# An unread fp32 product and four unread transposes at three places of a TensorE-bound kernel

## The chip, the cores and the metric

The kernel runs on one core of one Trainium2 chip. The metric is the device time of one execution in microseconds. A core has TensorE (PE, matrix products, with its weight loads listed apart as PEld), VectorE (DVE), ScalarE (ACT), GpSimd (POOL) and SyncE (SP), which here issues the DMAs.

## The reference

Two blocks on 256 tokens of width 1024, all fp32. The first has modulated feed-forward layers around a mixer that joins a short convolution and grouped-query attention; the second has an even layer (mLSTM heads and stick-breaking heads) and an odd layer (pooling windows, a mixing product, a gated projection):

```python
def reference(...):
    x = first_block(x, c, ctx, c_ctx, ...)      # 256 latent and 256 context tokens
    return second_block(x, ...)

def first_block(...):
    x = x + 0.5 * ml[2] * swiglu(modulate(rms_norm(x, norm1_g), ml[0], ml[1]), ffn1_w_in, ffn1_w_out)
    ...
    o_l = latent_attention(q_l, k_all, v_all)
    x = x + ml[5] * merge_branches(y_conv_l, o_l, gt_l, w_branch_conv, w_branch_attn, w_out)
    x = x + 0.5 * ml[8] * swiglu(modulate(rms_norm(x, norm3_g), ml[6], ml[7]), ffn2_w_in, ffn2_w_out)
    return rms_norm(x, final_g)

def odd_layer(...):
    ...
    y = (mixed * silu(z)) @ w_out
    return x + rmsnorm(y, post_g)
```

## The kernel before

Activations are kept transposed: features on the 128 partitions, tokens in the columns. Every large product is a `gemm`: two output tiles of 128 features from a strip of 256 weight columns, over `nk` slices of 128 features. The weights come in chunks of up to four slices (512 KB) through a ring `W` of eight buffers by SyncE. Each chunk is split into a high and a low part: ScalarE writes the high part `WH` (L1458), VectorE the rest `WL` (L1863). The activations are split in the same way (`XHB` and `XLB`, `GH` and `GL`, `OH` and `OL`, `YH` and `YL`, `RH` and `RL`). A slice is then three matmuls of 128x128 weights with 256 moving columns: high by high (L1038), high weights by low activations (L1039), low weights by high activations (L1040), 48 for a gemm with `nk` = 8 and 96 for one with `nk` = 16. They go to four PSUM banks in turn (0 to 3).

A planner (`Plan`) writes one list of steps, and each engine's program walks through it and does its share of each step. `prog` is a list of calls that make these steps; `gemm` and `call` append to it. Small work (attention, heads) is written as generators in `self.back`, which `tick` takes turns with, twice for each chunk. It uses the PSUM banks 4 to 6 in rotation: `bank` hands out the next one with the semaphore value at which the last user freed it, and TensorE waits on that value before the step.

TensorE works in the order of the list. Around the three places that order is: the attention is drained (`drain`), then the four gemms `ma` (attention branch, from 642.5 us), the four gemms `res` (w_out, to 688 us), a norm with some unread products of constants that bridge it (`warm`, L1057), then the second feed-forward block (`ffn(2, ...)`, from 694 us to 886 us: pairs of gemms `fa2` and `fb2`, and `fx2`); much later, from 1299.5 us, the four gemms `p1` (output projection of the odd layer, `nk` = 16), and the final norm.

Two steps of the attention have the shapes of the added ones: `score` (L1142), one fp32 product with 512 moving columns, and `turn` (L1147), four fp32 transposes of 128x128 into one bank. `gather` (L1154) is four fp32 products with 256 columns. An fp32 product appears in the trace as two records, a transpose as one.

```python
                elif s.kind == "turn":
                    pe.wait_ge(S["ap"], s.a + 1)
                    for c in range(4):
                        mm = pe.transpose(ps[:, c * 128:c * 128 + 128], TS[:, s.a % 3, c * 128:c * 128 + 128], con("id"))
                    mm.then_inc(S["atp"], 1)
```

Of the kernel before, what the change touches and what calls it, by code (L numbers as in the profile page):

```python
# [122 lines left out]
class Plan:  # L123
# [30 lines left out]
    def bank(self, freed):  # L154
        b = 4 + self.uses % 3
        self.uses += 1
        before = self.bank_free.get(b)
        self.bank_free[b] = freed
        return b, before

    def load(self, src, nk, freed):
        self.loads.append((src, nk, freed))
        return len(self.loads) - 1
# [364 lines left out]
    def build(self):  # L528
# [56 lines left out]
        self.call(self.drain)  # L585
        for i in range(4):
            self.gemm("ma", i, w["w_branch_attn"], 0, 8, 256 * i, (0, T), first=i == 0)
        self.call(self.stats, "s3")
        for i in range(4):
            self.gemm("res", i, w["w_out"], 0, 8, 256 * i, (0, T), first=i == 0, norm=i == 3)  # L590
# [37 lines left out]
        for g in range(4, 8):  # L628
            c = 5128 + 256 * (g - 4)
# [39 lines left out]
        self.call(self.stats, "s7")  # L669
        for i in range(4):  # L670
            self.gemm("p1", i, w["w_out_c_2"], 0, 16, 256 * i, (0, T), first=i == 0, norm=i == 3)
        self.call(self.post, 1)

    def ended(self, *name):
# [14 lines left out]
    def ffn(self, n, win, wout, cols):  # L689
        a, b = cols  # L690
        for f0, f1 in ((0, 12), (12, 22)):
            for f in range(2 if n == 1 and f0 == 0 else f0, f1, 2):
                self.gemm(f"fa{n}", f, win, 0, 8, f * 128, cols, first=f == 0)
                self.gemm(f"fb{n}", f, win, 0, 8, DFF + f * 128, cols)
            if f0 == 0:
                self.call(lambda: self.step("gates", a=n))
            else:
                self.call(self.ended, "hx", n)
                self.call(self.stats, "s2" if n == 1 else "s4")
            for m in range(0, 8, 2):  # L700
                if n == 1 and f0 == 12 and m == 6:
                    self.halves(wout, f0 * 128, f1 - f0, m * 128)
                    continue
                self.gemm(f"fx{n}", m, wout, f0 * 128, f1 - f0, m * 128, (0, b - a), g=f0, first=m == 0)
            self.call(self.ended, "fx", n, f0)
# [79 lines left out]
    def gates(self, bank):  # L785
        self.step("g0", bank=bank)
        for _ in range(5):
            yield
        self.step("g1", bank=bank)
        for _ in range(3):  # L790
            yield
        self.step("g2")
        for _ in range(8):
            yield
        b, f = self.bank(("att", 1))
        self.step("g4", bank=b, free=f)
        self.ready.add("att")
# [45 lines left out]
def build_program(nc, w, out):  # L843
    with ExitStack() as ctx:
# [12 lines left out]
        def sbuf(st, name, shape, dt=F32):  # L857
            return st.enter_context(nc.sbuf_tensor(name, shape, dt))

        V = sbuf(ctx, "V", [128, NVEC])  # L860
        C = sbuf(ctx, "C", [128, NCON])
# [62 lines left out]
        def con(name, a=0, b=None, rows=128):  # L924
            s, e = CON[name]
            return C[0:rows, s + a:(e if b is None else s + b)]
# [36 lines left out]
        @block.sync  # L963
        def _(sp):
            sp.dma_start(X[:, :, 256:512], w["xt"].rearrange("(k p) t -> p k t", p=128)).then_inc(SI[2], 16)
            sp.dma_start(X[:, :, 0:256], w["ctxt"].rearrange("(k p) t -> p k t", p=128)).then_inc(SI[3], 16)
            for i, (src, m, _) in enumerate(plan.loads):
                if i >= WR:
                    for name, v in plan.loads[i - WR][2]:
                        sp.wait_ge(S[name], v)  # L970
                sp.dma_start(W[:, i % WR, 0:m, 0:src.shape[2]], src).then_inc(SW[i % WR], 16)
                if i == 19:
                    for v, acc in enumerate((AC0, AC1)):
                        sp.dma_start(acc[:, :, :], w["cc"][v:v + 1, :].partition_broadcast(128)
                                     .rearrange("p o (t c) -> p (o t) c", t=4)).then_inc(SI[4 + 2 * v], 16)
                    sp.dma_start(C[:, EARLY:NCON], w["consts"][:, EARLY:NCON]).then_inc(SI[5], 16)
            for k in range(8):
                sp.wait_ge(S["pst"], 8 + k + 1)
                sp.dma_start(out[k * 128:k * 128 + 128, :], X[:, k, 256:512]).then_inc(S["out"], 16)
            sp.wait_ge(S["out"], 16 * 8)  # L980

        @block.tensor
        def _(pe):
# [78 lines left out]
            for s in seq:  # L1062
                ps = P[:, s.bank, :]
# [4 lines left out]
                elif s.kind == "s1":  # L1068
                    pe.wait_ge(SI[1], 16)
                    pe.wait_ge(S["sf"], 4 * s.a + 4)  # L1070
                    for t in range(2):
                        c = 128 * t
# [5 lines left out]
                elif s.kind == "mm":  # L1078
                    pe.wait_ge(S["sc"], 1)
                    for r in range(2):  # L1080
                        n = s.load + r
                        pe.wait_ge(SW[n % WR], 16 * (n // WR + 1))
                        for k in range(4):
                            mm = pe.matmul(ps[32 * k:32 * k + 32, 0:256], SCP[:, 4 * r + k, :], W[:, n % WR, k, :],  # L1084
                                           start=r == 0, stop=r == 1)
                        mm.then_inc(S["mm"], 1)
                elif s.kind == "mt":
                    pe.wait_ge(S["mr"], 2 * s.a + 2)
                    for g in (1, 0):
# [4 lines left out]
                elif s.kind == "os":  # L1094
                    sq0, pa0, on0, nb = stat["s2"]
                    c = slice(256 - 256 * s.a, 512 - 256 * s.a)
# [24 lines left out]
                elif s.kind == "qa":  # L1121
                    for i in range(4):
                        n = 4 * s.a + i
                        pe.wait_ge(S["qs"], n + 1)
                        pe.matmul(ps[0:4, 0:T], con("hot", 4 * i, 4 * i + 4), SQ[:, n % 3, T * (n // 3 % 2):T * (n // 3 % 2) + T], start=i == 0,
                                  stop=i == 3).then_inc(S["qh"], 1)
# [22 lines left out]
                elif s.kind == "gather":  # L1149
# [3 lines left out]
                    for c in range(4):  # L1153
                        mm = pe.matmul(ps[:, 0:T], VV[:, c, kv * 128:kv * 128 + 128], PT[:, s.a % 2, c, :],  # L1154
                                       start=c == 0, stop=c == 3)
# [21 lines left out]
                elif s.kind == "m0":  # L1177
# [6 lines left out]
                              stop=True).then_inc(S["m1p"], 1)  # L1184
# [28 lines left out]
                elif s.kind == "k0":  # L1213
                    n = s.a - 4
# [9 lines left out]
                elif s.kind == "k1":  # L1224
                    n = s.a - 4
# [8 lines left out]
                elif s.kind == "k2":  # L1234
                    n = s.a - 4
# [11 lines left out]
        @block.gpsimd  # L1247
        def _(pool):
            for name in ("s2", "s3", "s4", "s5", "s7"):
                sq0, pa0, _, _ = stat[name]  # L1250
                n = WIDE[name]
                for k in range(1, 6):
                    pool.wait_ge(S["sq"], sq0 + k + 1)
                    if k > 1:
                        pool.wait_ge(S["pa"], pa0 + k - 1)
                    pool.tensor_tensor(SQ[:, 0, 0:n], SQ[:, 0, 0:n], SQ[:, 1 + (k - 1) % 2, 0:n], ALU.add) \  # L1256
                        .then_inc(S["pa"], 1)

        @block.scalar
        def _(act):  # L1260
# [189 lines left out]
            for s in seq:  # L1450
# [81 lines left out]
                elif s.kind == "qs":  # L1532
                    act.wait_ge(S["on"], stat["s2"][2] + 6)
                    for i in range(4):
                        ap, _, _, (name, v) = head(s.a, i)
                        n = 4 * s.a + i
                        act.wait_ge(S[name], v)
                        if n >= 6:
                            act.wait_ge(S["qh"], n - 5)
                        act.activation(SQ[:, n % 3, T * (n // 3 % 2):T * (n // 3 % 2) + T], ap, ACT.Square).then_inc(S["qs"], 1)  # L1540
# [713 lines left out]
```

## Time and profile before

| | us |
|---|---|
| median of 3 runs | 1351.93 |
| lowest, highest | 1349.24, 1356.86 |
| profiled execution | 1357.65 |
| its span | 1355.86 |
| TensorE busy in it | 1320.6 |
| VectorE, ScalarE busy | 906.0, 648.1 |

The span is the time from the first to the last instruction of the profiled execution. Matmuls are pipelined, and a record lasts from its start to a modelled end, so neighbouring records overlap; the distance from one start to the next tells what a matmul costs. The page names lines of the kernel as L1039. The granted clock is that of TensorE, 1.00 for 2.4 GHz and 0.50 for 1.2 GHz.

### The profile page before, as it was taken

To read this page: it belongs to the slowest core of one execution; us is meant where nothing else is said; L and a number is where in the kernel's file an instruction comes from. 1 tells how busy PE (TensorE), PEld (TensorE's weight loads), DVE (VectorE), ACT (ScalarE), POOL (GpSimd) and SP (SyncE) were. 2 spreads that over 40 slices of the span, in tenths; PEclk is the share of its full clock that TensorE was granted. 3 is DMA by queue.
4 is the path that set the end of the run, shared out by engine and by line. 5 is a ranking of instruction groups with operands and counts; after the bars stand their busy time and mean duration, and the time that the engine had idled before them with its cause. 6 is when DMAs were issued, how large, how long until landed. Compare 5 with 4: busy or idle time off the path is not lost.

```text
span 1355.9 us, 23439 instructions
## 1 busy us (share of the span) xinstructions
PE 1320.6 (97%) x9310; PEld 1212.0 (89%) x9310; DVE 906.0 (67%) x1462; ACT 648.1 (48%) x1025; POOL 30.3 (2%) x29
## 2 busy tenths in 40 slices
PE   6999999999999999999999999999999999999996
PEld 3688888888898889999999999998999999999996
DVE  3577875646658487654775555678886665689873
ACT  4433222223236335554454444566665765556552
POOL 0000000000010000000000000200000000100000
PEclk6999999999999999999999999999999999999998
DMA  8755656465544334444546655565546455437650
GB/s 303 262 166 188 206 193 218 161 216 184 176 153 156 109 113 152 127 150 148 183 142 186 199 175 172 155 188 157 169 135 193 126 166 177 140 119 215 196 172 32
DMA packets 201404, 229.69 MB, mean 169 GB/s; under 512 B 7120, under 2 KB 191696, under 8 KB 201296
## 3 DMA queue, kind: packets, MB, share of 16 engines
q1 hardware_dynamic: 201008, 227.90, 53.0%
q8 instruction: 75, 1.23, 0.4%
q14 instruction: 33, 0.27, 0.1%
q10 hardware_dynamic: 288, 0.29, 0.1%
HBM read 227.11 MB, written 1.05 MB: 168 GB/s over the span
## 4 chain that ended last, share of the span: by engine, by line
PE 88%; DVE 7%; ACT 3%; issue 2%; DMA 0%; DVEq 0%; ACTq 0%
PE P L1038 26%; PE P L1039 25%; PE P L1040 25%; DVE WL L1863 1%; PE P L1044 1%; PE P L1046 1%; PE P L1045 1%; PE P L1154 1%; DVE TS L1791 1%; PE P L1142 1%; PE P L1000 1%; PE P L1084 1%; DVE TS L1663 1%; ACT WH L1458 1%; PE P L1131 1%
## 5 line engine op out<-in xcount | busy, mean ns | idle before, releaser
L1038 PE MATMUL P<-XHB,WH 128*128 128x256 f32 (+1 forms) x1808 | 561.2, 310 | 7.5 <-DVE XLB L1675 3.7
L1039 PE MATMUL P<-XLB,WH 128*128 128x256 f32 (+1 forms) x1808 | 545.9, 302 | 0.0
L1040 PE MATMUL P<-XHB,WL 128*128 128x256 f32 (+1 forms) x1808 | 545.7, 302 | 0.0
L1863 DVE TENSOR_TENSOR WL<-W,WH 128x1024 fp32r<-128x1024 f32 x358 | 431.1, 1222 | 100.1 <-ACT WH L1458 99.9
L1458 ACT ACTIVATE WH<-W 128x1024 fp32r<-128x1024 f32 x358 | 368.7, 1041 | 251.4 <-PE P L1040 175.8
L1038 PEld LDWEIGHTS P<-XHB,WH 128*128 128x128 f32 x1808 | 341.9, 189 | 35.4 <-issue 14.0
L1039 PEld LDWEIGHTS P<-XLB,WH 128*128 128x128 f32 x1808 | 340.7, 188 | 18.0 <-issue 3.1
L1040 PEld LDWEIGHTS P<-XHB,WL 128*128 128x128 f32 x1808 | 340.6, 188 | 14.6
L1038 PE MATMUL P<-GH,WH 128*128 128x256 f32 (+1 forms) x372 | 122.0, 328 | 0.0
L1040 PE MATMUL P<-GH,WL 128*128 128x256 f32 (+1 forms) x372 | 121.5, 327 | 0.0
L1039 PE MATMUL P<-GL,WH 128*128 128x256 f32 (+1 forms) x372 | 121.5, 326 | 0.0
L1739 DVE TENSOR_TENSOR TS<-TS,P 128x512 f32<-128x512 f32 (+1 forms) x44 | 24.3, 554 | 83.0 <-PE P L1040 83.0
L1038 PEld LDWEIGHTS P<-GH,WH 128*128 128x128 f32 x372 | 70.7, 190 | 6.4 <-issue 0.2
L1039 PEld LDWEIGHTS P<-GL,WH 128*128 128x128 f32 x372 | 70.0, 188 | 6.4 <-issue 0.2
L1040 PEld LDWEIGHTS P<-GH,WL 128*128 128x128 f32 x372 | 70.0, 188 | 6.0
L1930 DVE CUSTOM_DVE_ANT_0 W<-W,AC,V 128x1024 f32<-128x1024 f32 x56 | 72.7, 1298 | 0.0
L1327 ACT ACTIVATE GH<-TS 128x512 fp32r<-128x512 f32 (+1 forms) x44 | 23.1, 526 | 92.3 <-DVE TS L1739 92.3
L1321 ACT ACTIVATE TS<-P 128x512 f32<-128x512 f32 (+1 forms) x44 | 21.4, 491 | 86.5 <-PE P L1040 86.5
L1256 POOL TENSOR_TENSOR SQ<-SQ 128x256 f32<-128x256 f32 (+1 forms) x25 | 30.1, 1205 | 1303.8 <-ACT SQ L1282 1302.7
L1749 DVE SCALAR_TENSOR_TENSOR X<-P,GM,X 128x256 f32<-128x256 f32 x48 | 21.5, 480 | 53.5 <-PE P L1040 53.4
L1044 PE MATMUL P<-WH,XHB 128*128 128x256 f32 x160 | 45.6, 285 | 1.1 <-DVE WL L1863 1.0
L1046 PE MATMUL P<-WH,XLB 128*128 128x256 f32 x160 | 44.5, 278 | 0.0
(302 smaller groups left out, 1813.8 us busy)
## 6 DMA issues: line engine op xcount, KB each, us to landing
W<-in_ffn_w_in SPq DMA_DIRECT2D x88, 512.0 KB, 4.8
W<-in_w_in_ab SPq DMA_DIRECT2D x72, 512.0 KB, 4.5
W<-in_w_modt SPq DMA_DIRECT2D x56, 512.0 KB, 3.9
W<-in_w_in SPq DMA_DIRECT2D x52, 512.0 KB, 3.6
W<-in_ffn_w_out SPq DMA_DIRECT2D x40, 512.0 KB, 4.6
W<-in_w_in_c SPq DMA_DIRECT2D x32, 512.0 KB, 4.3
W<-in_w_mod SPq DMA_DIRECT2D x16, 512.0 KB, 7.1
W<-in_w_out_ab SPq DMA_DIRECT2D x16, 512.0 KB, 4.4
```

The costliest lines, as they stand in the source:

```text
L1038: pe.matmul(o, h[:, k, c], xh[:, kk, a:b], start=kk == 0, stop=False)
L1039: pe.matmul(o, h[:, k, c], xl[:, kk, a:b], start=False, stop=False)
L1040: mm = pe.matmul(o, l[:, k, c], xh[:, kk, a:b], start=False, stop=kk == gm.nk - 1)
L1044: pe.matmul(o, xh[:, kk, c], h[:, k, :], start=kk == 0, stop=False)
L1046: mm = pe.matmul(o, xl[:, kk, c], h[:, k, :], start=False, stop=kk == gm.nk - 1)
L1256: pool.tensor_tensor(SQ[:, 0, 0:n], SQ[:, 0, 0:n], SQ[:, 1 + (k - 1) % 2, 0:n], ALU.add) \
L1327: act.activation(GH[m][:, f % 12, :], TS[:, f % NS, 0:n], ACT.Copy).then_inc(S[f"hh{m}"], 1)
L1458: act.activation(h, a, ACT.Copy).then_inc(S["wh"], 1)
L1739: dve.tensor_tensor(TS[:, f % NS, 0:n], TS[:, f % NS, 0:n], ps, ALU.mult).then_inc(S[f"hm{m}"], 1)
L1749: up = dve.scalar_tensor_tensor(X[:, k, ca:cb], ps[:, ca - a:cb - a], GM[:, m - 1, v, k:k + 1], X[:, k, ca:cb], ALU.mult, ALU.add)
L1863: dve.tensor_tensor(l, a, h.bitcast(F32), ALU.subtract).then_inc(S["wl"], 1)
L1930: td = dve.tensor_tensor_reduce(a if v == s.c - 1 else JK[:, :, :], a, (AC0, AC1)[v][:, :, :], 1.0, vec("bmod", 8 * g + k), ALU.mult, ALU. ...
```

## The change

A new step `settle` is put into TensorE's order at three places: after the first gemm `ma`, after the first pair `fa2` and `fb2`, and after the first gemm `p1`. It looks up the next small bank without taking it, waits until that bank was freed, and writes an fp32 product of 512 constant columns into it, and then four transposes of the constant `one`. Nothing reads what it writes. It has no work for any other engine.

```diff
+    def settle(self):
+
+        b = 4 + self.uses % 3
+        self.step("settle", bank=b, free=self.bank_free.get(b))
 
     def load(self, src, nk, freed):
...
         for i in range(4):
             self.gemm("ma", i, w["w_branch_attn"], 0, 8, 256 * i, (0, T), first=i == 0)
+            if i == 0:
+                self.call(self.settle)
...
         for i in range(4):
             self.gemm("p1", i, w["w_out_c_2"], 0, 16, 256 * i, (0, T), first=i == 0, norm=i == 3)
+            if i == 0:
+                self.call(self.settle)
...
                 self.gemm(f"fa{n}", f, win, 0, 8, f * 128, cols, first=f == 0)
                 self.gemm(f"fb{n}", f, win, 0, 8, DFF + f * 128, cols)
+                if n == 2 and f == 0:
+                    self.call(self.settle)
...
+                elif s.kind == "settle":
+                    pe.matmul(ps, con("one"), C[:, 0:512], start=True, stop=True)
+                    for c in range(4):
+                        pe.transpose(ps[:, c * 128:c * 128 + 128], con("one"), con("id"))
```

## Rows read from the trace of the kernel before

**Rows 1.** The page: engine totals, and the chain that ended last by engine.

```profile
PE 1320.6 (97%) x9310; PEld 1212.0 (89%) x9310; DVE 906.0 (67%) x1462; ACT 648.1 (48%) x1025; POOL 30.3 (2%) x29
...
PE 88%; DVE 7%; ACT 3%; issue 2%; DMA 0%; DVEq 0%; ACTq 0%
```

**Rows 2.** TensorE's waits from 640 us on: who for whom, us in total, times, longest.

```profile
PE P L1038 <- DVE WL L1863: 2.6, 3, 1.3
...
PE P L1038 <- DVE XLB L1675: 1.1, 1, 1.1
...
PE P L1044 <- DVE WL L1863: 1.0, 1, 1.0
```

**Rows 3.** Table by stretch: length, busy us and records (x) of each engine, granted clock, DMA share, GB/s.

```profile
648.00:686.00 38.00, 38.00 (x325) 38.00 (x324) 29.75 (x44) 21.02 (x30) 5.40 (x5) 1.00 0.57 170
...
706.00:886.00 180.00, 180.00 (x1526) 179.52 (x1525) 105.01 (x134) 89.60 (x132) 7.27 (x5) 1.00 0.59 182
...
1218.00:1299.00 81.00, 81.00 (x715) 81.00 (x716) 74.75 (x154) 49.69 (x85) 0.00 (x0) 1.00 0.67 204
...
1305.00:1342.00 37.00, 37.00 (x328) 36.99 (x327) 12.25 (x10) 16.06 (x25) 4.11 (x5) 1.00 0.20 64
```

**Rows 4.** The second matmul's line in six stretches: ns min/median/max, first and last start us.

```profile
L1039 PE MATMUL P<-YL,WH x59: 281/281/281, 665.3 to 685.8; 128*128 128x256 f32 x59
...
L1039 PE MATMUL P<-XLB,WH x321: 281/281/281, 705.8 to 852.8; 128*128 128x256 f32 x161
...
L1039 PE MATMUL P<-XLB,WH x35: 276/276/282, 892.9 to 910.0; 128*128 128x256 f32 x35
...
L1039 PE MATMUL P<-XLB,WH x23: 281/281/281, 1050.0 to 1057.8; 128*128 128x256 f32 x23
...
L1039 PE MATMUL P<-XLB,WH x174: 276/276/276, 1218.8 to 1291.2; 128*128 128x256 f32 x174
...
L1039 PE MATMUL P<-RL,WH x89: 276/276/276, 1311.0 to 1340.9; 128*128 128x256 f32 x89
```

**Rows 5.** TensorE in order of time around one score product: start us, us, line, count.

```profile
561.50 0.28 PE L1040 MATMUL P<-XHB,WL 128*128 128x256 f32 x1
561.62 1.02 PE L1142 MATMUL P<-K,Q 128*128 128x512 f32 x2
562.08 0.68 PE L1038 MATMUL P<-YH,WH 128*128 128x256 f32 x1
562.60 0.28 PE L1039 MATMUL P<-YL,WH 128*128 128x256 f32 x1
```

**Rows 6.** The same order of time around four transposes of the attention.

```profile
565.12 0.28 PE L1040 MATMUL P<-YH,WL 128*128 128x256 f32 x1
565.23 0.60 PE L1147 MATMUL P<-C,TS 128*128 128x128 f32 x4
565.59 0.37 PE L1038 MATMUL P<-YH,WH 128*128 128x256 f32 x1
565.79 0.29 PE L1039 MATMUL P<-YL,WH 128*128 128x256 f32 x1
```

**Rows 7.** The second matmul's line in five short stretches of the attention, columns as in group 4.

```profile
L1039 PE MATMUL P<-XLB,WH x8: 278/281/281, 558.9 to 561.4; 128*128 128x256 f32 x8
...
L1039 PE MATMUL P<-YL,WH x8: 276/276/281, 562.6 to 565.0; 128*128 128x256 f32 x8
...
L1039 PE MATMUL P<-YL,WH x7: 276/276/279, 566.2 to 568.2; 128*128 128x256 f32 x7
...
L1039 PE MATMUL P<-XLB,WH x4: 281/281/281, 569.4 to 570.5; 128*128 128x256 f32 x4
...
L1039 PE MATMUL P<-XLB,WH x8: 277/281/281, 574.4 to 576.9; 128*128 128x256 f32 x8
```

**Rows 8.** Granted clock early and in the rest, columns as in group 3.

```profile
11.50:34.50 23.00, 13.93 (x72) 7.91 (x73) 9.92 (x25) 8.62 (x16) 0.00 (x0) 0.50 0.82 303
...
46.00:1340.00 1294.00, 1283.03 (x9109) 1186.68 (x9102) 880.92 (x1400) 629.84 (x991) 30.12 (x25) 1.00 0.53 167
```

## The prediction

> **What bounds the kernel now.** Read first the engine totals and the chain of waits: TensorE is busy 97% of the span and the chain lies on it for 88% [rows 1]. Then its waits from 640 us on, where all three places of the change lie: after the attention no wait group is above 2.6 us, and the three largest sum to 4.7 us of some 715 us [rows 2]. Then the table by stretch. The reader is to see that TensorE is busy in every microsecond of all four stretches, while VectorE is busy 105 of 180 us in the second feed-forward block and 12 of 37 in the last projection, and the DMA share is 0.59 and 0.20 [rows 3]. So what is added to TensorE there has no idle time to fall into, and what it saves is not held back by another engine.
>
> The same table holds a second thing, which the busy share hides. The feed-forward stretch passes 1526 matmul records in 180 us, 118.0 ns each; the stretch from 1218 us passes 715 in 81 us, 113.3 ns each [rows 3]. It is the same instruction (128x128 weights, 256 columns) at the same granted clock of 1.00. The durations name the two cadences: every one of 321 records of the second matmul in the feed-forward stretch lasts 281 ns, every one of 174 after 1218 us lasts 276 ns; the attention's projection and w_out run at 281, the last projection at 276 [rows 4]. A cadence, once taken, holds for hundreds of matmuls. I call them slow (118) and quick (113.3); they differ by about 4.5 ns, 4%. VectorE is busy 74.8 of 81 us in the quick stretch and still does not slow it [rows 3].
>
> **The change part by part.** Nothing is removed or moved. Three times TensorE gets one step: a wait on the semaphore that freed the bank it peeks at, one product of 512 columns, four transposes. The step does not advance the bank counter, starts no DMA, increments no semaphore, and VectorE, ScalarE and the planner's turns do not know it.
>
> The wait: the bank was freed three bank uses ago, in the attention or, for the last place, in the stick-breaking heads; none of them lies within 10 us of its place. Cost nothing. Queued behind it is only the next chunk's matmuls; were the wait late, they would all be late.
>
> The product: the score product of the attention has its shape, and is two records. The last ordinary matmul before it starts at 561.50, the second after it at 562.60 [rows 5]: 1.10 us for two ordinary steps plus the product, so 1.10 - 2 x 0.118 = 0.86 us. The transposes: from 565.12 to 565.79 is 0.67 us [rows 6], less 2 x 0.113 = 0.44 us. Together 1.30 us a place, three places **+3.9 us**, all on the path. The bounds of this are narrow: 0.43 to 0.45 us for the transposes by other instances, and 1.3 us each time unless the product and transposes overlap differently back to back, so 3.7 to 4.1 us.
>
> What the step does to the cadence is the open cost. After the score product at 561.6 the kernel went from slow (281 before) to quick (276 after); after the transposes at 565.2, it stayed quick; after the score product at 568.4 it went to slow; after the transposes at 573.8 it stayed slow [rows 7]. Read in this way from 503 to 627 us, of which these five stretches are a part, all 16 score products reverse the cadence (6 from slow to quick, 10 from quick to slow), and the 16 groups of transposes keep it where it was quick (5 of 5) and leave it quick in 5 and slow in 6 of 11 where it was slow. So at a slow place the likeliest course is: the product makes it quick, the transposes leave it. At a quick place the product makes it slow, and the transposes leave it slow by 6 in 11. Product and transposes back to back are seen nowhere, and the course at a slow place is an estimate from these counts, 7 in 10.
>
> What the cadence is worth, at 4.5 ns a matmul. First place, after the first 48 matmuls of the attention's projection (648.2 us) up to 686.2: about 323 matmuls, slow before, **-1.45 us** if quick. Second place, after 96 matmuls of the feed-forward block (704.8 us) up to 886.3: about 1535 matmuls, all slow before, **-6.9 us**. Third place, after 96 matmuls of the last projection (1310.5 us) up to 1341.7: 275 matmuls, already quick, nothing if it stays, **+1.2 us** if it turns slow, which I take, by 6 in 11. The cadences are those of [rows 3, 4]. Bounds of all this against the profiled execution: from -8.4 us (both turn quick, the last stays) to +1.2 us (neither turns, the last does).
>
> The Trainium skill (TensorE: Matmul & The Clock Gate, section "Back-to-back issue gap") gives for a warm matmul of N columns N / 2.4 + 2.5 ns, 109 ns for 256. The rows show 113.3 and 118.0, so it does not hold to the nanosecond here, and has one cadence where the trace has two. By it the step could change nothing but add itself, the second rival below.
>
> **Against which time.** The profiled execution took 1357.65 us (span 1355.86 and 1.8 around it), the median of three is 1351.93, between 1349.24 and 1356.86. Four times stand in two groups: 1349.2 and 1351.9, and 1356.9 and 1357.7, whose means are 6.7 us apart, which is what the feed-forward block's cadence is worth (6.9). I read this as one more sign that it is drawn anew in each execution, in the wait for the first normed tiles, and that the profiled one drew slow. From the profiled execution: 1357.65 + 3.9 - 1.45 - 6.9 + 1.2 = 1354.4. From the median, if it had the block quick before and has it quick after: 1351.93 + 3.9 - 1.45 + 1.2 = 1355.6. I take 1355.0.
>
> **The rivals.**
> - Larger gain: the distance of 5.7 us between profiled execution and median is not the cadence, the block is slow in every run before, and the step turns it. 1351.93 + 3.9 - 8.35 = 1347.5, the last projection staying quick. For it: 1500 matmuls without one change of cadence. Against it: the two groups of times.
> - Toll alone: the cadences are drawn as before, or have nothing to do with the step. 1351.93 + 3.9 = 1355.8. For it: waits and other small products also change the cadence, which is 276 ns from 893 us and 281 from 1050 us with no score product between [rows 4]. If the unread products did not run at all it would be 1351.9; nothing in the kernel before shows an unread product being dropped.
> - Slower: the step pins the feed-forward block to slow, as 6 groups of transposes did. 1357.65 + 3.9 = 1361.6, and 1362.8 with the last projection slow too; with the first place quick 1360.2. It decides in the first ten matmuls after the step at 704.8 us: from there 1535 matmuls cost 6.9 us over the quicker runs. For it: a quick block goes through the reversing product too, and would come out slow; against it: where the block is drawn slow, the product makes it quick first, and all five such groups of transposes kept it.
> - Clock: the granted clock was 0.50 (1.2 GHz) over the 23 us from 11.5 us, when TensorE was busy 13.9 of them, and 1.00 (2.4 GHz) in all of the rest [rows 8]. A fall of such a length would cost half of it, 1355 + 11.5 = 1366.5. Against it: the sixteen groups of transposes and the score products lie in the stretch at 1.00. The Trainium skill (TensorE: Matmul & The Clock Gate, "Part 4: PE-mode transpose") says that transposes do not count as activity of TensorE for the clock; by that rule, the 0.44 us in each place could only count against it.
>
> **How the numbers follow.** Chances: forecast 0.40, larger gain 0.20, toll alone 0.14, slower 0.24, clock 0.02. The range from 1347 to 1362 holds all but a part of the slower case and of the larger gain, and the clock, and takes in whatever the later stages draw (the heads from 1050 us are slow too [rows 4]). 0.5% is 6.8 us, about what a measurement of this kernel can tell from no change. Faster by more needs under 1345.2: only the larger gain with a lucky draw in a later stage, or a median before that comes out high, 0.12. Slower by more needs over 1358.7: the slower case, most of it, and the clock, 0.24. The rest, 0.64, is within it.
>
> **What would show it.** In the profile after: three groups of one product (two records) and four transposes, each about 1.3 us between its neighbours; the durations 276 instead of 281 on the second matmul's line from the second place to the end of the feed-forward block, and some 113.3 ns a matmul there; the same from 648 to 686 us; the granted clock 1.00. If the block stays at 281 ns in the profile, the forecast's cadence step is wrong; if the product and transposes take clearly over 1.4 us or a wait stands before them, the toll is. If single executions of the changed kernel still fall into two groups 6.7 us apart, the step does not set the cadence.

## The result

| | before | after |
|---|---|---|
| median of 20 runs each, us | 1357.17 | 1360.72 |
| lowest, highest | 1349.24, 1363.64 | 1356.79, 1364.79 |
| profiled execution | 1357.65 | 1362.17 |

The changed kernel takes 1.0034 times as long (95% interval 1.0018 to 1.0050): 3.6 us slower by the medians, and within 0.5%. The median of the kernel before is 5.2 us above that of the three runs on which the prediction stood. Of its 20 times 5 lie between 1349 and 1352, 10 between 1355.9 and 1359.1 and 5 between 1361.7 and 1363.7; 17 of the 20 of the changed kernel lie between 1359.3 and 1362.2, and none under 1356.

The page of the changed kernel, engine totals and the chain by engine, beside [rows 1]:

```profile
PE 1324.5 (97%) x9328; PEld 1215.2 (89%) x9328; DVE 906.4 (67%) x1462; ACT 648.3 (48%) x1025; POOL 30.3 (2%) x29
...
PE 86%; DVE 9%; ACT 3%; issue 2%; DMA 1%; SPq 0%; DVEq 0%; ACTq 0%
```

TensorE has 3.9 us more of busy time (1324.5 for 1320.6) and 18 matmul records more: three times a product of two records and four transposes.

TensorE in order of time around the step in the second feed-forward block (start us, us, line, count):

```profile
704.75 0.28 PE L1051 MATMUL P<-XHB,WL 128*128 128x256 f32 x1
704.87 1.02 PE L1099 MATMUL P<-C 128*128 128x512 f32 x2
705.72 0.60 PE L1101 MATMUL P<-C 128*128 128x128 f32 x4
706.08 0.36 PE L1049 MATMUL P<-XHB,WH 128*128 128x256 f32 x1
706.28 0.28 PE L1050 MATMUL P<-XLB,WH 128*128 128x256 f32 x1
```

From 704.75 to 706.28 is 1.53 us for the step and two ordinary matmuls. With 2 x 0.115 for those, the step costs 1.30 us, as [rows 5, 6] gave it. It starts 0.12 us after its neighbour; there is no wait in front.

The table by stretch, beside [rows 3], with the last stretch cut to what lies behind the third step (length, busy us and records of each engine, granted clock, DMA share, GB/s):

```profile
648.00:686.00 38.00, 38.00 (x333) 37.70 (x332) 29.58 (x44) 21.31 (x30) 5.41 (x5) 1.00 0.57 175
...
706.00:886.00 180.00, 180.00 (x1525) 179.52 (x1524) 104.19 (x132) 89.10 (x131) 7.27 (x5) 1.00 0.58 180
...
1218.00:1299.00 81.00, 81.00 (x690) 81.00 (x689) 72.45 (x149) 47.99 (x81) 0.00 (x0) 1.00 0.63 196
...
1314.00:1346.00 32.00, 32.00 (x280) 31.55 (x279) 9.80 (x8) 13.49 (x21) 4.10 (x5) 1.00 0.07 20
```

In the same 38 us behind the first place 333 matmuls start now, 325 before. In the same 180 us of the feed-forward block it is 1525 for 1526: no gain. In 81 us of the odd layer that hold no step, it is 690 for 715. The clock is 1.00 in all.

The second matmul's line (L1050 here), ns min/median/max with first and last start, on both sides of each of the three places, beside [rows 4]: first place before and behind, second before and behind, the odd layer, third before and behind.

```profile
L1050 PE MATMUL P<-OL,WH x13: 281/281/281, 642.9 to 647.2; 128*128 128x256 f32 x13
...
L1050 PE MATMUL P<-OL,WH x48: 276/276/283, 648.8 to 664.8; 128*128 128x256 f32 x48
...
L1050 PE MATMUL P<-XLB,WH x20: 276/276/282, 698.2 to 704.6; 128*128 128x256 f32 x20
...
L1050 PE MATMUL P<-XLB,WH x318: 281/281/281, 707.0 to 852.9; 128*128 128x256 f32 x159
...
L1050 PE MATMUL P<-XLB,WH x176: 281/281/287, 1217.7 to 1293.7; 128*128 128x256 f32 x176
...
L1050 PE MATMUL P<-RL,WH x31: 281/281/281, 1302.9 to 1313.5; 128*128 128x256 f32 x31
...
L1050 PE MATMUL P<-RL,WH x91: 276/276/283, 1315.1 to 1345.8; 128*128 128x256 f32 x91
```

This is the reading that matters. At the first place 281 becomes 276, as forecast. The second place is met at 276, while the profiled execution of the kernel before had 281 there, and becomes 281 for the rest of the block. The odd layer is slow long before the third step, where [rows 4] had it quick, and the third step turns it to 276.

### The profile page after: what moved, and what is told of

The parts are those of the page before. It is cut to its first block, busy times and chain, and to the rows that moved or that the text cites. A ratio compares the mean times of both kernels' runs of the same rounds, so it can differ in the third digit from the quotient of the medians.

```text
span 1360.4 us, 23475 instructions
## 1 busy us (share of the span) xinstructions
PE 1324.5 (97%) x9328; PEld 1215.2 (89%) x9328; DVE 906.4 (67%) x1462; ACT 648.3 (48%) x1025; POOL 30.3 (2%) x29
## 4 chain that ended last, share of the span: by engine, by line
PE 86%; DVE 9%; ACT 3%; issue 2%; DMA 1%; SPq 0%; DVEq 0%; ACTq 0%
PE P L1049 25%; PE P L1050 25%; PE P L1051 25%; DVE WL L1878 2%; DVE TS L1806 1%; PE P L1169 1%; PE P L1055 1%; PE P L1057 1%; PE P L1056 1%; PE P L1157 1%; PE P L1011 1%; DMA W<-in_w_mod 1%; DVE TS L1678 1%; ACT WH L1473 1%; PE P L1095 1%
## 5 line engine op out<-in xcount | busy, mean ns | idle before, releaser
L1050 PE MATMUL P<-XLB,WH 128*128 128x256 f32 (+1 forms) x1808 | 546.3, 302 | 0.0
L1050 PEld LDWEIGHTS P<-XLB,WH 128*128 128x128 f32 x1808 | 341.9, 189 | 17.9 <-issue 3.1
L1050 PE MATMUL P<-GL,WH 128*128 128x256 f32 (+1 forms) x372 | 121.5, 327 | 0.0
L1050 PEld LDWEIGHTS P<-GL,WH 128*128 128x128 f32 x372 | 70.7, 190 | 6.3 <-issue 0.2
```

The source lines that it names most:

```text
L1050: pe.matmul(o, h[:, k, c], xl[:, kk, a:b], start=False, stop=False)
```

## Where the time went

Two more rows of the changed kernel, the first matmul of the attention's projection and of the last projection (ns, first and last start):

```profile
L1049 PE MATMUL P<-OH,WH x64: 276/276/367, 641.7 to 664.7; 128*128 128x256 f32 x64
...
L1049 PE MATMUL P<-RH,WH x128: 276/276/469, 1302.4 to 1347.8; 128*128 128x256 f32 x128
```

Between the two profiled executions, which are 4.5 us apart: the projection starts at 641.7 instead of 642.5 us, 0.8 us earlier, before any step. The early stretch at the lower clock was shorter: over 11.5 to 34.5 us the granted clock is 0.55 here and was 0.50 [rows 8]. From there to the first matmul of the last projection it is 660.7 us instead of 657.1, 3.6 more. Of these, two steps cost 2.6; the quick projection and w_out give 1.45 back; the 59 quick matmuls ahead of the second step give 0.3; the slow odd layer costs 3.2 (some 720 matmuls at 4.5 ns from 1218 us on). That is 4.0, and 0.4 less comes out of the stretches between. From the first matmul of the last projection on it is 1.7 more: 1.3 for the step, 0.43 for the 96 matmuls ahead of it that ran slow. The feed-forward block behind its step costs what it cost, since it was slow before and is slow now. So between these two executions the steps themselves are 3.9 us, and the rest is a change of cadence here and there, some of it far from any step.

## The experiments

Twelve kernels in three groups; each group shares its runs of the kernel before. In what follows, block is the second feed-forward block, slow is 281 and quick 276 ns on the second matmul's line, and P and T are the product and the four transposes. The low group is the times under 1354 us; next to it the kernel before has none between 1352 and 1354. It had 45 of 105 times in the low group over all jobs. The expectations letter their theories: A, a step reverses the cadence; B, it draws it anew; C, it is a toll alone; D, transposes (later the whole step) leave the block slow; E, any step there does; F, the place decides; G, the length of the product decides.

**The kernel before, once more.** No edit.

> The kernel before, unchanged, profiled once more. If the cadence of the second feed-forward block (1540 matmuls) and of the odd layer (1090 matmuls) are drawn in each execution, this one's time is 1350.7 us with both quick, plus 6.9 with the block slow, plus 4.9 with the odd layer slow (1357.6, 1355.6 or 1362.5), within 1 us. If the cadence has nothing to do with the spread of the single times, the time doesn't match the durations.

It took 1350.15 us. The block's stretch and the odd layer's in the table by stretch, then the second matmul's line in w_out, in the block and in the last projection:

```profile
699.00:873.00 174.00, 174.00 (x1538) 174.00 (x1537) 105.93 (x132) 91.69 (x133) 7.28 (x5) 1.00 0.61 188
...
1211.00:1292.00 81.00, 81.00 (x717) 81.00 (x716) 74.93 (x154) 49.40 (x84) 0.00 (x0) 1.00 0.66 206
...
L1039 PE MATMUL P<-YL,WH x60: 281/281/281, 664.4 to 685.3; 128*128 128x256 f32 x60
...
L1039 PE MATMUL P<-XLB,WH x338: 276/276/276, 699.0 to 846.2; 128*128 128x256 f32 x169
...
L1039 PE MATMUL P<-RL,WH x97: 276/276/276, 1300.0 to 1332.7; 128*128 128x256 f32 x97
```

The block passes 1538 matmuls in 174 us, 113.1 ns each, where [rows 3] show 118.0; its durations are 276 where [rows 4] show 281. w_out ahead of it was at 281 in both. The time is 7.5 us below the profiled execution of [rows 3, 4], of which the block is 6.9 (an estimate, 1535 matmuls at 4.5 ns); another 0.8 lies ahead of the attention's projection, which starts at 641.7 instead of 642.5 us, with a granted clock of 0.55 instead of 0.50 over 11.5 to 34.5 us. It is the same program. So the distance between the times near 1350 and near 1357 is mostly whether the block runs quick or slow. The group near 1362 would be both the block and the odd layer slow: an estimate from some 1090 matmuls at 4.5 ns, 4.9 us, since no profiled execution of this kernel had the odd layer slow. The prediction's median of three was drawn from that spread.

**The first place alone.** From the changed kernel:

```diff
             self.gemm("p1", i, w["w_out_c_2"], 0, 16, 256 * i, (0, T), first=i == 0, norm=i == 3)
-            if i == 0:
-                self.call(self.settle)
...
-                if n == 2 and f == 0:
-                    self.call(self.settle)
```

> The step stands behind the attention alone. Theory A: the projection goes from 281 to 276 ns at the step and w_out runs at 276 ns to its end, 1.45 us less for 1.3 us of step, so no change there. If the quick w_out is what lets the second feed-forward block begin quick, the block is quick to its end (276 ns) and the kernel is about 6.9 us faster than executions with a slow block, 1350 to 1353 us with a narrow spread. Theory B: the block draws as it does in the kernel before, two groups of times, median 1357. Theory C: 281 ns throughout and plus 1.3 us.

1350.62 us median of 12 beside 1351.39 for the kernel before in the same job, ratio 1.0001 (0.9979 to 1.0023). 9 of 12 in the low group, 14 of 23 for the kernel before. The line before the step, in w_out, and in the block:

```profile
L1046 PE MATMUL P<-OL,WH x15: 281/281/282, 642.9 to 647.9; 128*128 128x256 f32 x15
...
L1046 PE MATMUL P<-YL,WH x60: 275/276/277, 666.2 to 686.3; 128*128 128x256 f32 x60
...
L1046 PE MATMUL P<-XLB,WH x338: 275/276/277, 699.9 to 847.1; 128*128 128x256 f32 x169
```

Slow becomes quick at the step, and the step's 1.30 us and the 1.45 us that it gives back cancel, as both theory A and the prediction had it. The 10 profiled executions without a step at this place run it at 281 ns up to 694 us. That a quick w_out makes the block begin quick is not shown: 9 of 12 and 14 of 23 can't be told apart.

**The block's place alone**, twice. From the changed kernel:

```diff
             self.gemm("ma", i, w["w_branch_attn"], 0, 8, 256 * i, (0, T), first=i == 0)
-            if i == 0:
-                self.call(self.settle)
...
             self.gemm("p1", i, w["w_out_c_2"], 0, 16, 256 * i, (0, T), first=i == 0, norm=i == 3)
-            if i == 0:
-                self.call(self.settle)
```

> The step stands at the second feed-forward block alone. Theory A (the step reverses the cadence it meets): the block's matmuls before the step and the 1500 after it have opposite durations, 276 then 281 ns or 281 then 276; the attention's projection and w_out stay at 281 ns as in the kernel before. Single times still lie in two groups some 7 us apart, with the groups' shares exchanged, and the median is 1.3 us plus or minus some 3 us from before. Theory B (any interruption draws the cadence anew, by chance): before and after the step are as often alike as opposite. Theory C (the step is a toll and has nothing to do with the cadence): the same cadence on both sides of the step, and plus 1.3 us.

> The whole step at the second feed-forward block alone, as before, for more executions. Theory D (it leaves the block slow whatever it meets): profile 281 ns behind the step, nearly all times at 1358 to 1360 or, with the odd layer slow too, 1363 to 1364; fewer than one in ten near 1352. Theory B (a fresh draw): about half of them near 1352 or 1357.

The first gave 1358.67 us median of 6, ratio 1.0052 (1.0035 to 1.0069), the second 1358.54 us median of 11, ratio 1.0026 (1.0006 to 1.0045). All 17 times lie between 1357.7 and 1360.1. The kernel before had 14 of 23 and 9 of 27 in the low group in the same two jobs. The line before and behind the step in the first; the second has 281 ns on both sides too:

```profile
L1046 PE MATMUL P<-XLB,WH x18: 280/281/282, 700.9 to 706.9; 128*128 128x256 f32 x18
...
L1046 PE MATMUL P<-XLB,WH x319: 280/281/282, 708.9 to 855.2; 128*128 128x256 f32 x160
```

Slow before, slow behind. Theory A, the reversal, falls. So does theory B as it was put, with no time of 17 in the low group. What holds is that with this step in this place the low group is gone, and that this place alone loses as much by its ratios (1.0026 and 1.0052) as all three together (1.0034).

**The product alone, all three places.**

```diff
                 elif s.kind == "settle":
                     pe.matmul(ps, con("one"), C[:, 0:512], start=True, stop=True)
-                    for c in range(4):
-                        pe.transpose(ps[:, c * 128:c * 128 + 128], con("one"), con("id"))
```

> At all three places the product alone, without the four transposes: 0.86 us a place, 2.6 us in all. Theory A, by which the product is what reverses: at each place the durations change from 276 to 281 ns or from 281 to 276, as after the score products, and the time is 1.3 us below the changed kernel's 1360.7, about 1359.4. If the transposes were needed for the reversal, the places show the same duration on both sides.

1352.65 us median of 12, ratio 1.0004 (0.9983 to 1.0024), 7 of 12 in the low group. The line in w_out, before and behind the second place, before and behind the third:

```profile
L1050 PE MATMUL P<-YL,WH x60: 275/276/277, 666.3 to 686.3; 128*128 128x256 f32 x60
...
L1050 PE MATMUL P<-XLB,WH x17: 275/276/277, 700.0 to 705.4; 128*128 128x256 f32 x17
...
L1050 PE MATMUL P<-XLB,WH x319: 275/276/281, 707.3 to 848.1; 128*128 128x256 f32 x160
...
L1050 PE MATMUL P<-RL,WH x16: 281/281/282, 1301.9 to 1307.2; 128*128 128x256 f32 x16
...
L1050 PE MATMUL P<-RL,WH x90: 275/276/282, 1309.4 to 1339.7; 128*128 128x256 f32 x90
```

Quick behind the first place, quick on both sides of the second, slow to quick at the third. In the block the product reverses nothing. This execution took 1356.15 us with a quick block and a slow odd layer. So a time outside the low group does not by itself tell of a slow block: by an estimate from this time, less the 1.15 us that these steps cost net, such an execution of the kernel before takes 1355.0 us, or 1356.2 where the last projection stays slow too. Eight of its 105 times lie from 1354.2 to 1356.2.

**The transposes alone, all three places.**

```diff
                 elif s.kind == "settle":
-                    pe.matmul(ps, con("one"), C[:, 0:512], start=True, stop=True)
                     for c in range(4):
                         pe.transpose(ps[:, c * 128:c * 128 + 128], con("one"), con("id"))
```

> At all three places the four transposes alone, 0.44 us a place, 1.3 us in all. Theory A, by which transposes keep a quick cadence and turn a slow one in about half of the cases: a place met at 276 ns stays at 276; a place met at 281 ns can go either way. With the block met quick in most executions it stays quick, and the median is about 1352 to 1355 us. Theory B: a place met quick becomes slow about as often as not, median about 1358.

1358.56 us median of 6, ratio 1.0052 (1.0035 to 1.0069), all six between 1358.0 and 1360.2. The same five stretches:

```profile
L1050 PE MATMUL P<-YL,WH x60: 275/276/277, 665.3 to 685.3; 128*128 128x256 f32 x60
...
L1050 PE MATMUL P<-XLB,WH x19: 280/281/282, 698.3 to 704.7; 128*128 128x256 f32 x19
...
L1050 PE MATMUL P<-XLB,WH x319: 280/281/282, 706.2 to 852.4; 128*128 128x256 f32 x160
...
L1050 PE MATMUL P<-RL,WH x20: 275/277/277, 1302.0 to 1308.5; 128*128 128x256 f32 x20
...
L1050 PE MATMUL P<-RL,WH x91: 280/281/282, 1310.0 to 1341.8; 128*128 128x256 f32 x91
```

Quick behind the first place, slow on both sides of the second, quick to slow at the third. The median fits the 1358 of theory B and not the 1352 to 1355 of theory A. So transposes do not keep a quick cadence in every place, as the five groups in the attention did. From these six times I formed theory D, that the transposes pin the block slow.

**The product alone, the block's place alone.** All that follow have their steps in the block only. The diffs are against the kernel with the block's place alone, but for the next one's:

```diff
-                    for c in range(4):
-                        pe.transpose(ps[:, c * 128:c * 128 + 128], con("one"), con("id"))
```

> At the second feed-forward block alone, the product without the transposes (0.86 us). Theory D (the transposes pin the block slow, whatever it was; the product does not): the block stays free to be quick or slow, single times lie in two groups near 1351.5 and 1358.5, as in the kernel before. Theory E (any step at this place pins the block slow): 281 ns after the step and all single times between 1357.5 and 1360.

1353.81 us median of 12, ratio 1.0000 (0.9971 to 1.0029); 6 of 12 in the low group beside 17 of 35 for the kernel before in this job. Before and behind the step:

```profile
L1046 PE MATMUL P<-XLB,WH x17: 281/281/281, 700.0 to 705.7; 128*128 128x256 f32 x17
...
L1046 PE MATMUL P<-XLB,WH x318: 281/281/281, 708.0 to 853.9; 128*128 128x256 f32 x159
```

Slow stays slow here, quick stayed quick in the kernel above. The product leaves the block's cadence alone and both groups of times remain. Theory E falls.

**Transposes and product 96 matmuls apart.** Against the kernel before; `s.a` is the `f` with which the step is called, so the transposes come first:

```diff
+                if n == 2 and f in (0, 2):
+                    self.call(self.settle, f)
...
+                    if s.a:
+                        pe.matmul(ps, con("one"), C[:, 0:512], start=True, stop=True)
+                    else:
+                        for c in range(4):
+                            pe.transpose(ps[:, c * 128:c * 128 + 128], con("one"), con("id"))
```

> At the second feed-forward block alone, the four transposes behind the first pair of gemms and the product behind the second pair, with 96 ordinary matmuls between them, as such pairs lie in the attention. Theory D: 281 ns between the two, 276 ns behind the product, times narrow near 1351 to 1352.5. If the product's reversal holds only in the attention, 281 ns behind it in some executions and 276 in others, two groups of times.

1351.85 us median of 12, ratio 1.0001 (0.9978 to 1.0024), 9 of 12 in the low group. Before the transposes, between the two, behind the product:

```profile
L1046 PE MATMUL P<-XLB,WH x18: 276/276/277, 699.4 to 705.2; 128*128 128x256 f32 x18
...
L1046 PE MATMUL P<-XLB,WH x30: 276/276/277, 706.7 to 716.5; 128*128 128x256 f32 x30
...
L1046 PE MATMUL P<-XLB,WH x287: 276/276/281, 718.4 to 848.3; 128*128 128x256 f32 x144
```

276 throughout. The transposes met the block quick and left it quick, so theory D falls in this form too. The same P and T as in the changed kernel, for the same 1.3 us, leave the block free once 96 ordinary matmuls stand between them: the 9 low times show that, and the profile that each part let a quick block pass.

**Product last, and the whole step one pair later.**

```diff
+                    for c in range(4):
+                        pe.transpose(ps[:, c * 128:c * 128 + 128], con("one"), con("id"))
                     pe.matmul(ps, con("one"), C[:, 0:512], start=True, stop=True)
-                    for c in range(4):
-                        pe.transpose(ps[:, c * 128:c * 128 + 128], con("one"), con("id"))
```

```diff
-                if n == 2 and f == 0:
+                if n == 2 and f == 2:
```

> At the second feed-forward block alone, the four transposes first and the product last. Theory D with the reversal of the score products: the transposes leave a state that is slow, the product behind them reverses it, so the block is quick in all executions: 276 ns behind the step, narrow times near 1350 to 1352. Theory E: 281 ns and 1358 to 1360.

> The whole step at the second feed-forward block alone, one pair of gemms (96 matmuls) later. Theory D: slow again behind the step, single times all near 1358 to 1360. Theory F (the outcome belongs to this very place in the program, not to the step's make): the later place comes out otherwise, quick in all executions (1350 to 1353) or mixed.

Product last: 1360.52 us median of 12, ratio 1.0031 (1.0000 to 1.0061), 2 of 12 in the low group. Before and behind the step:

```profile
L1046 PE MATMUL P<-XLB,WH x18: 276/276/277, 700.2 to 706.0; 128*128 128x256 f32 x18
...
L1046 PE MATMUL P<-XLB,WH x319: 281/281/281, 708.3 to 854.6; 128*128 128x256 f32 x160
```

One pair later: 1358.52 us median of 12, ratio 1.0046 (1.0024 to 1.0068), 1 of 12 in the low group. Before and behind:

```profile
L1046 PE MATMUL P<-XLB,WH x48: 281/281/281, 700.0 to 716.6; 128*128 128x256 f32 x48
...
L1046 PE MATMUL P<-XLB,WH x287: 281/281/281, 718.9 to 853.9; 128*128 128x256 f32 x144
```

With the product last a block met quick became slow, the second such case after the changed kernel itself. Slow in place of the quick that theory D expected. The later place is slow as well, which gives theory F no support. Neither order nor place frees it, but now 3 of 24 times are low, so it is no law for each execution.

**A shorter product**, of 384 columns as here, and of 256 in a second kernel.

```diff
-                    pe.matmul(ps, con("one"), C[:, 0:512], start=True, stop=True)
+                    pe.matmul(ps[:, 0:384], con("one"), C[:, 0:384], start=True, stop=True)
```

> The whole step at the second feed-forward block alone, with a product of 384 columns instead of 512 (0.22 us less). Theory D (the kind of step pins the block slow): times as with 512 columns, 1358 to 1359.5, less 0.2 us. Theory G (the outcome hangs on how long the interruption is, to the nanosecond): another outcome, quick in most executions (near 1351.5) or a mixture.

> The same with 256 columns (0.43 us less than with 512). Theory D: 1357.5 to 1359. Theory G: quick in most executions, near 1351.3, or a mixture, and not the same as with 384.

384 columns: 1357.66 us median of 11, ratio 1.0014 (0.9998 to 1.0029), all between 1357.4 and 1358.0. 256 columns: 1357.24 us median of 11, ratio 1.0010 (0.9994 to 1.0026), all between 1356.2 and 1358.1. Before and behind the step, 384 columns and then 256:

```profile
L1046 PE MATMUL P<-XLB,WH x18: 281/281/281, 699.4 to 705.4; 128*128 128x256 f32 x18
...
L1046 PE MATMUL P<-XLB,WH x319: 281/281/281, 707.6 to 853.9; 128*128 128x256 f32 x160
```

```profile
L1046 PE MATMUL P<-XLB,WH x18: 281/281/281, 699.4 to 705.4; 128*128 128x256 f32 x18
...
L1046 PE MATMUL P<-XLB,WH x319: 281/281/281, 707.3 to 853.6; 128*128 128x256 f32 x160
```

The length of the product changes nothing but its own price. Theory G gets no support; but both profiled executions met the block slow, so they do not show what these steps do to a quick one.

**The profiled executions together.**

| place | step | met slow, left | met quick, left |
|---|---|---|---|
| first | P+T, P or T | quick in 4 of 4 | |
| second, or a pair later | P and T adjoining, any order or length | slow in 5 of 5 | slow in 2 of 2 |
| second, or a pair later | P or T alone | slow in 2 of 2 | quick in 3 of 3 |
| third | P+T or P | quick in 2 of 2 | |
| third | T | | slow in 1 of 1 |

## Why the prediction was right, and where it was wrong

The measured 1360.72 us lies in the range of 1347 to 1362 and within 0.5% of the kernel before, as the likeliest class had it. The steps that led there did not all hold, and two things were luck. The class: by the prediction's own bounds, over 1358.7 us was "slower by more", and 1360.72 is 0.65% above the 1351.93 from which it reckoned; it is within 0.5% only because the median before rose to 1357.17 with more runs. The difference: the prediction's sum from the median adds 3.9 - 1.45 + 1.2 = 3.65 us, and 3.6 was measured, but not by these terms, as the second and the third place show.

- **TensorE is the bound, nothing hides the step.** Held. The three steps are 3.9 us of TensorE's time, the chain stays on it, and no wait stands in front.
- **The toll of 1.30 us a place.** Held to the hundredth in the trace.
- **Two cadences, 4.5 ns a matmul, 6.9 us for the block.** Held: the kernel before profiled once more had the block quick and came out 7.5 us lower.
- **First place, -1.45 us.** Held: quick in 4 of 4 profiled executions with a step there and slow in 10 of 10 without, and 325 matmuls became 333 in the same stretch.
- **Second place, -6.9 us by 7 in 10.** This is the step that failed. The prediction carried the counts of the attention over: the product reverses (16 of 16), the transposes keep. In the block the product reversed nothing (3 of 3), and product and transposes side by side left it slow in 7 of 7. What took place in all seven is the rival "slower: the step pins the feed-forward block to slow": the term -6.9 us was 0 in the profiled execution, and instead of a gain the low group of times was lost.
- **Third place, +1.2 us.** Wrong sign in the profiled execution: it was met slow and left quick. The odd layer draws its cadence too, which the single profile, where it was quick, did not tell. What product and transposes together do to a quick last projection, no profiled execution shows.
- **The time before.** The prediction took the median of three, 1351.93, as the base and read it as an execution with a quick block. Executions with a quick block do take that time, but the three runs were an unusual draw: with 20 runs the median is 1357.17. The rival with the steady slow block gave 1360.2 to 1362.8, in which 1360.72 falls; the forecast's 1355.0 is 5.7 us short.
- **Clock.** The rival did not take place: the granted clock of the changed kernel is 1.00 from 46 to 1345 us, with all three groups of transposes in it.
- **The formula.** The Trainium skill (TensorE: Matmul & The Clock Gate, section "Back-to-back issue gap") calls N / 2.4 + 2.5 ns the gap of an isolated matmul and says that a stream with weight loads departs from it, which the prediction left out. So 109 ns beside 113.3 and 118.0 does not test it. No term of the sum hangs on it.

The measured difference can be made up by an estimate from these numbers: the three steps cost 3.9 us, the first place gives 1.45 back, and the block is taken as slow always instead of in three executions of four at most (5 of 20 times lay in the low group), which is 0.25 x 6.9 = 1.7 at least. Sum +4.2 us, beside 3.9 between the means of the 20 runs each (1360.9 and 1356.9) and 3.6 between the medians. The third place is left out: it gave back 1.2 us by the cadence where it was met slow, and what it does where it is met quick is not shown.

**What stays open.** That a step with P and T adjoining leaves the block slow rests on 7 profiled executions and on the low group: 3 of 83 times lie in it (0 of 59 for the changed kernel, the block's place alone twice, and 384 and 256 columns; 3 of 24 for the product last and the later place), beside 45 of 105 for the kernel before. Three doubts remain.

First, only two of the seven met the block quick. In three kernels of one job (the step again, 384 and 256 columns) the block was entered slow, with the same distances from start to start in its first matmuls, so the entry may be fixed for a program in some surroundings, and part of the 59 may be owed to that and not to the step. Against it, the kernel before drew both ways in that same job (9 of 27 low). The six times of the transposes alone point to such a fixed entry: none is low, though the transposes in the block kept a slow block slow in that kernel and a quick one quick in another.

Second, a quick block with a slow odd layer is not in the low group. From the lowest time above the low group, 1354.2, and the 1356.2 estimated above it would stand between 1355.5 and 1357.5 us with the step at the block's place, an estimate. None of the 17 times there is under 1357.6. But the 1356.79 of the changed kernel and the lowest times with 256 columns (from 1356.16) may be such executions, so that the block of the changed kernel is slow in every execution is not shown.

Third, a rule that tells from the starts of the last matmuls what a step leaves behind was not found: the same product turned slow into quick in the attention and in both projections, and not in the block.

No kernel tried made the block quick in all executions, and none beats the kernel before: the best by its ratio, the product at the block's place alone, is at 1.0000, and the first place alone and the parts 96 matmuls apart are at 1.0001.

## What to carry to other kernels

Where matmuls stand back to back, divide a stretch by its count of matmuls: two executions of one program can differ by 4% there while busy shares and the clock are alike, and three runs do not give the median of such a kernel. In this kernel a piece of unread work was a sure toll with an uncertain effect on that cadence, and counts taken in one part of it did not hold in another. Where the wanted effect is a draw, look at single times by group, not at the median.

## What the runs showed of the hardware

- The same matmul (128x128 weights, 256 columns) at the granted clock of 1.00 has two stable spacings, 113.1 to 113.3 and 118.0 ns, with durations of 276 and 281 ns, each held for over 1500 matmuls. Which one an undisturbed stretch gets differs between executions of the same program: the block of the kernel before was slow in one profiled execution and quick in the other, 6.9 us apart.
- Short unread fp32 work of 0.44 to 1.3 us can change it for the rest of a dense stretch: at the first place from slow to quick in 4 of 4 profiled executions, for over 300 matmuls; in the feed-forward block, with product and transposes adjoining, from quick to slow in 2 of 2, for over 1500 matmuls.
- The 512-column fp32 product cost 0.86 us (by itself in the kernel with the product alone) and four transposes 0.44 us (in that with the transposes alone) on constants, the same as on the attention's data [rows 5, 6].
